# Who begins the transfers of the experts' down weights: ScalarE, two experts ahead, in place of SyncE

## What is computed

```python
def moe_ffn(h, w_router, router_bias, w_gate, w_up, w_down, ws_gate, ws_up, ws_down):
    scores = jax.nn.sigmoid((t @ w_router).astype(jnp.float32))
    ...
    _, eidx = lax.top_k(jnp.where(emask, biased, -jnp.inf), TOP_K)      # 8 of 64 experts
    ...
        hg = jnp.einsum('nd,edf->nef', t, w_gate[sl])                   # 1024 -> 256
        hu = jnp.einsum('nd,edf->nef', t, w_up[sl])
        hw = jax.nn.silu(hg) * hu * combine[:, sl, None]
        routed = routed + jnp.einsum('nef,efd->nd', hw, w_down[sl])     # 256 -> 1024
    shared = (jax.nn.silu(t @ ws_gate) * (t @ ws_up)) @ ws_down
    return (routed + shared).reshape(B, S, D)
```

## Time and profile before

| | |
|---|---|
| three runs | 1072.33, 1073.07, 1077.84 us (median 1073.07) |
| the profiled execution | 1075.1 us, its span 1073.3 us |
| mean granted TensorE clock | 0.958 |
| busy | PE 89%, DVE 83%, ACT 57%, POOL 27% |

### The profile page before, as it was taken

One profiled execution on the slowest core, in us unless ns is written; L12 is line 12 of the kernel. 1 busy time (PEld: TensorE's weight loads), 2 busy tenths in 40 slices (PEclk: granted clock), 3 DMA queues, 4 the chain that ended last, 5 costly groups with the idle time before them and its releaser, 6 DMA issues.

```text
span 1073.3 us, 14279 instructions
## 1 busy us (share of the span) xinstructions
PE 958.2 (89%) x4323; PEld 749.9 (70%) x4324; DVE 891.8 (83%) x1276; ACT 613.2 (57%) x961; POOL 286.6 (27%) x181
## 2 busy tenths in 40 slices
PE   1899998997999889899998899989898998899895
PEld 1654764776887568677787787778776777777674
DVE  4888779354548779999999899999998999899894
ACT  4215442555022157667677687767676777677672
POOL 1000132400000104332434243342433333324341
PEclk9999999588998999999999999999999999999997
DMA  9995222000044488999999999999999999999992
GB/s 353 396 381 191 76 79 107 1 1 1 36 181 181 137 307 287 364 343 350 343 329 343 337 336 363 350 364 336 325 358 352 317 346 370 348 340 370 340 293 38
DMA packets 93681, 286.27 MB, mean 267 GB/s; under 512 B 19496, under 2 KB 20008, under 8 KB 92752
## 3 DMA queue, kind: packets, MB, share of 16 engines
q1 hardware_dynamic: 71424, 248.04, 62.3%
q0 software_dynamic: 19056, 36.89, 13.9%
q10 hardware_dynamic: 3168, 0.94, 0.4%
HBM read 282.50 MB, written 37.88 MB: 298 GB/s over the span
## 4 chain that ended last, share of the span: by engine, by line
DMA 49%; PE 31%; DVE 10%; issue 6%; ACT 2%; POOL 1%; POOLq 0%; SPq 0%; DVEq 0%; ACTq 0%
DMA out<-oute,src_tab 44%; PE bank L613 6%; PE bank L574 4%; PE bank L575 4%; PE bank L576 4%; DMA xe<-h_rows,src_tab 4%; PE bank L698 2%; PE bank L777 2%; PE bank L715 2%; DVE q_sb L1350 1%; PE bank L794 1%; DVE gu_low L1503 1%; DMA x_sb<-in_x 1%; PE bank L706 1%; POOL out L530 1%
## 5 line engine op out<-in xcount | busy, mean ns | idle before, releaser
L1503 DVE TENSOR_TENSOR gu_low<-w_gu,gu_high 128x1024 fp32r<-128x1024 f32 x256 | 301.4, 1219 | 8.1 <-ACT gu_high L1115 3.4
L1115 ACT CAST gu_high<-w_gu 128x1024 fp32r<-128x1024 f32 x256 | 256.7, 1055 | 59.9 <-PE bank L576 54.8
L530 POOL DMA_INDIRECT out<-oute,src_tab x64 | 144.6, 2259 | 424.8 <-DMA out<-oute,src_tab 310.2
L574 PE MATMUL bank<-gu_high,xeT_high 128*128 128x512 f32 x512 | 208.2, 407 | 2.3 <-DVE xeT_low L1503 2.3
L576 PE MATMUL bank<-gu_high,xeT_low 128*128 128x512 f32 x512 | 202.1, 395 | 0.0
L575 PE MATMUL bank<-gu_low,xeT_high 128*128 128x512 f32 x512 | 201.8, 394 | 0.0
L1503 DVE TENSOR_TENSOR d_low<-w_d,d_high 128x1024 fp32r<-128x1024 f32 x128 | 150.5, 1218 | 0.0
L1121 ACT CAST d_high<-w_d 128x1024 fp32r<-128x1024 f32 x128 | 128.2, 1054 | 12.4 <-PE bank L576 12.4
L810 PE MATMUL bank<-ident,xe 128*128 128x128 f32 x512 | 73.9, 290 | 47.8 <-DMA xe<-h_rows,src_tab 47.5
L574 PE MATMUL bank<-d_high,hwT_high 128*128 128x512 f32 x256 | 110.2, 430 | 6.5 <-DVE hwT_low L1503 6.5
L524 POOL DMA_INDIRECT xe<-h_rows,src_tab x64 | 99.7, 1558 | 53.3 <-DVE src_tab L1575 27.9
(11 more groups left out here) (283 smaller groups left out, 1294.0 us busy)
## 6 DMA issues: line engine op xcount, KB each, us to landing
w_gu<-in_w_exp_gate SPq DMA_DIRECT2D x128, 512.0 KB
w_gu<-in_w_exp_up SPq DMA_DIRECT2D x128, 512.0 KB
w_d<-in_w_exp_down SPq DMA_DIRECT2D x128, 512.0 KB
ada_w<-in_w_ada SPq DMA_DIRECT2D x8, 2048.0 KB
first_w<-in_w_ada SPq DMA_DIRECT2D x3, 2048.0 KB, 22.6
w_out_sb<-in_w_out SPq DMA_DIRECT2D x2, 2048.0 KB, 7.2
w_lat_sb<-in_w_in SPq DMA_DIRECT2D x1, 2688.0 KB, 23.2
x_sb<-in_x SPq DMA_DIRECT2D x1, 2048.0 KB, 13.4
```

What stands on the lines that cost most here:

```text
L530: pool.indirect_dma_start(out_rows, bass.IndirectOffsetOnAxis(ap=rows, axis=0), oute[i][:], None, bounds_check=last_row, oob_is_err=False, ...
L574: pe.matmul(dst, xh, wh, start=start, stop=False)
L1115: act.copy(gu_high[half][:, m], w_gu[half][i][:, m]).then_inc(gu_high_ok[half], 1)
L1503: return dve.tensor_tensor(low, whole, high.bitcast(F32), ALU.subtract)
```

## The change

SyncE no longer loads down weights. ScalarE begins the loads of experts 0 and 1 ahead of its first `gu_high`. In step E, right after `hwT_high` of E, it waits until VectorE has finished `d_low` of the same expert E, and begins the two transfers of E+2. The buffers, the sizes and the number of transfers are the same.

```diff
-            def load_down(e, i):
-                src = a["w_exp_down"][0, bass.ds(e, 1)].rearrange("o (p c) n -> p (o c) n", c=FC)
-                for j in range(FC):
-                    sp.dma_start(w_d[i][:, j], src[:, j]).then_inc(ld_d[i], 16)
-
-            def down_step(E):
-                wait(sp, d_low_ok, num(E, -1))
-                apart(sp, "sp")
-                load_down(num(E), E[1] % 2)
...
-                if not (E[0] is None and E[1] == 0):
-                    down_step(after(E, -1))
 
             every_expert(sp, step)
-            down_step((None, NE - 1))
...
+            def load_down(e, i):
+                src = a["w_exp_down"][0, bass.ds(e, 1)].rearrange("o (p c) n -> p (o c) n", c=FC)
+                for j in range(FC):
+                    act.dma_start(w_d[i][:, j], src[:, j]).then_inc(ld_d[i], 16)
...
             act.wait_ge(h2_ok, T)
+            load_down(0, 0)
+            load_down(1, 1)
             gate_up_high_of(0, (None, 0))
...
                 hidden_high(num(E))
+                if exists(E2):
+                    act.wait_ge(d_low_ok, num(E, 1))
+                    apart(act, "act")
+                    load_down(num(E2), E2[1] % 2)
                 if exists(E2) and not first(E):
                     gate_up_high_of(0, E2)
```

More of the change, by code:

```diff
@@ L324, in wait @@
                 eng.wait_ge(s, value)
-        apart_sem = {"sp": sem("sp_apart"), "pool": sem("pool_apart")}
+        apart_sem = {"sp": sem("sp_apart"), "pool": sem("pool_apart"), "act": sem("act_apart")}
         def apart(eng, name):
@@ L463, in extra @@
                 load_gate_up(e, 0, 1)
-                load_down(e, 0)
             n = extra_blocks(sp, extra)
@@ L1195, in extra @@
                 n = i + NE
+                act.wait_ge(d_mm, i + NE)
+                e = act.value_load(list_i[0:1, bass.ds(i, 1)], min_val=0, max_val=NE - 1)
+                apart(act, "act")
+                load_down(e, 0)
                 gate_up_high(0, 0, i * 32 + 32 * (EXTRA0 + 1), n)
```

## The result

The changed kernel takes 1161.76 us (median of 4, 1156.9 to 1175.25) against 1074.38 us before (4 runs). The ratio is 1.087, 95% interval [1.080, 1.093]: slower, by 87 us between the medians. The forecast was 1160 us, +87.

A forecast was written before the change was run, and what follows sets the result against it. VectorE was taken to bound the expert pass at 9.92 us a step, with about 42 us of late gathers on top. Terms 79.6 + 6 + 1 = +87 on the median of 1073.07 gave 1160 us, range 1140 to 1200.

The forecast's parts named there:

- The ring: Each expert step: VectorE `d_low`, ScalarE issues, ScalarE `gu_high`, VectorE `gu_low` in a closed chain; 2.0 us a step, +79.6 us.
- The length of the new piece: From `d_low` to `gu_low` in each step: 2.16 us where 0.26 was, so 1.90 lost, taken as 2.0.
- SyncE's part and the start of the transfers: SyncE losing two issues and a wait per expert is worth nothing; down-weight transfers start when they did.
- The late gathers: Expert rows landing late, about 42 us over the pass before; mostly hidden by longer steps, 0.1 a step kept, +6.
- the floor: Expert pass: VectorE's back-to-back work sets a least step of 9.92 us, against 10.61 measured before.
- The sum: Whole kernel: 79.6 + 6 + 1 = +87 us, giving 1160 us, 8% slower.
- the +1 for the start: Start of the pass and step 0: ScalarE's early issues ahead of its first `gu_high` and activation cost +1 us.
- Rival A: Expert pass: scatter and gather become the chain as down weights get their own queue; +122, 1195 us; chance 0.15.
- Rival B: ScalarE's issues in each step are nearly free, leaving 1.09 a step; +24, 1097 us; chance 0.05.
- Rival C: Expert pass: TensorE's clock falls from idling; at 0.75 a step of 12.6, 1194 us; chance 0.03.
- Rival D: Not slower: ScalarE's wait in each step costs nothing and the gathers profit; 1031 us; chance 0.02.
- Rival E: The change does not move the down-weight loads; 1073 us; chance 0.01.

The follow-up runs named there:

- wait_only: Kernel before, with ScalarE also waiting for `d_low` of the same expert where the change has it, all loads still begun by SyncE; ratio 1.027, 1093.90 us.
- after_half0: The change, with ScalarE's wait and two transfers placed behind `gu_high` of half 0 instead of ahead of it; ratio to the kernel before 1.013, 1085.19 us.
- the last four experiments: Four of the eight follow-up runs; the kernel before had a median of 1069.96 us beside them.
- half0_tiny: Kernel before, with ScalarE waiting for `d_low` and beginning two 4 KB transfers behind `gu_high` of half 0, SyncE still loading; ratio 1.003, 1074.65 us.
- one_ahead: The change, issuing in the same place but loading the next expert's down weights, not two ahead, behind an already met wait; ratio to before 1.027, 1099.52 us.
- one_transfer: The change, with one 1 MB transfer for each expert's down weights in place of two of 512 KB; ratio to the kernel before 1.051, 1124.87 us.

## Why the prediction was right, step by step

- *The ring.* Right, and shown: it appears with the wait alone (wait_only) and goes when the same lines stand behind the cast (after_half0). VectorE's idle time before `gu_low`, 120.7 us in 59 waits, lies in the 115 to 125 that were given. The mechanism and the amount are both as forecast.
- *The length of the new piece.* 2.0 us a step was sized a little low: 12.06 against 11.92. In the step shown it is 2.59 - 0.26 = 2.33, and on average 12.06 - 9.92 = 2.14. A pair of issues took 0.94 on average (0.82 to 1.35) where I had 0.81, and there is 0.1 to 0.2 behind them where I had 0.04. As a price: 0.34 a step for the wait over before (late gathers lost already set against it), then 0.55 and 0.56 for the issues.
- *SyncE's part and the start of the transfers.* As predicted, worth nothing; the first issue stands 0.24 behind `d_low`, SyncE's stood 0.16 behind.
- *The late gathers.* I kept 0.1 a step and they are gone, 3.7 us in all. That gives back 6 of the 8.6 us by which the ring was dearer. That all of the 42 us over the floor were late gathers said too much: before `xeT_low` VectorE stood 25.3 us behind ScalarE and 4.9 us with no releaser seen, some 30 us.
- *The sum.* The pass is 735.7 - 647.5 = 88.2 us longer, where 85.6 were predicted. The profiled spans differ by less, 81.8, mostly since expert 1 was reached 5.4 us sooner. That goes with TensorE's clock in attention, from 192 to 223, granted at 0.50 before and here at 0.78. In the five profiles with 0.50 to 0.56 there, expert 1 is reached at 404.6 to 405.2, in the five with 0.78 to 0.84 at 396.7 to 400.2, and kernels with the change's first loads and without them are in both groups. So the +1 for the start can't be seen. That the sum comes out within 1 us between the medians is luck in part: its errors of 8.6 and 6 offset one another, and the 29 runs of the kernel before that stand beside the last four experiments lie between 1059 and 1092. The row of the change:

```profile
192.00:223.00 31.00, 28.12 (x148) 22.83 (x148) 16.97 (x51) 16.38 (x60) 9.18 (x3) 0.78 0.01 2
```

- *Rival A.* Not in the change, whose longer step hides it: GpSimd waited 6 times for a scatter. Where the step is short (after_half0) something of it is seen: the down weights on their own queue go with later gathers and 1.3%, and that the queue is the reason is likely, not settled. The Trainium skill, "DMA: Bandwidth & Descriptors", section "Queues, rings and completion order", has each DMA engine take turns between the queues that have work. After_half0 against half0_tiny (60.7 and 51.5 us of waits for `xe`) goes the way of this rule, though turns as such are not seen.
- *Rival B.* Fell for the change (0.55 each), and held for one_ahead, where the issues run beside other work of ScalarE. Its step of 11.01 was near the 10.95 of wait_only, which has no issues.
- *Rival C.* The clock did fall, from 0.98 to 0.94 over the pass, which I had not expected. It cost nothing that can be seen: TensorE's 640.44 us in 731 still fit, and the step less its ring is 9.94, as good as the floor.
- *Rival D.* Fell. The Trainium skill's rule on the same page, "Issuing engines are not separate DMA queues", that only the issuing time is saved, agrees on the gain: none came. What decided was another thing, what ScalarE's own work had to wait for.
- *Rival E.* Fell: ScalarE's queue carries 68.06 MB.

## What to carry to other kernels

Before a transfer is moved to an engine that computes, ask what that engine must wait for to begin it, and what of its list stands behind that wait. Here the transfer was off the path and the engine had time to spare; a semaphore of the bounding engine, waited for just ahead of what that engine needs next, still closed a ring that no spare time could absorb. Behind a cast, or with a wait that was already met, the same issues took next to none of ScalarE's time. And with the DMA engines full, one late transfer put right went with another late one.

## What the runs showed of the hardware that was not expected

- ScalarE's DMA issues can run ahead of its compute. In one_ahead they ran at 709.65 during a cast that had begun at 709.36, two instructions ahead of their place in the list, and there every row of issues from 405 to 1055 began during one of ScalarE's compute instructions. With the change none did from 405 to 1130: behind an unmet wait they stand between the compute instructions, and each costs 0.55 to 0.6 us of ScalarE. A long row of issues costs time too: behind ten of them a copy stood idle for 8.06 us.
- TensorE's mean granted clock in the pass was 0.94 with the change, where TensorE stands idle for some 1.5 us a step, and 0.98 before; in wait_only it was 0.99 with some 1.0 us idle, in one_transfer 0.98 with some 1.3. What of the gaps matters was not tried.
- The time from issue to landing rose with the load of the DMA engines: for the down weights, begun by ScalarE in transfers of 512 KB, the median from 500 to 1000 was 6.1 us (4.2 to 10.2) with the change at a DMA share of 0.93, and 8.3 (5.0 to 12.2) in one_ahead at 0.98.
